# Second attention of a two-block transformer kernel: fp32 scores on 64 rows, the bias tile read from DRAM and added in the pass that takes the maximum, three SBUF tiles

## The reference

```python
def block(args):
    idx, qc = args
    q_pos = idx * Q_BLOCK + jnp.arange(Q_BLOCK)
    rel = k_pos[None, :] - q_pos[:, None]
    bias = rel_bias[t5_causal_bucket(rel)].astype(f32).transpose(2, 0, 1)
    s = jnp.einsum("bqhcd,bkhcd->bhcqk", qc, k).astype(f32) * scale
    s = s + bias[None, :, None]
    s = jnp.where(rel <= 0, s, NEG_INF_2)
    pm = jax.nn.softmax(s, axis=-1)
    attn = pm[:, :, 0] - lam * pm[:, :, 1]
    return jnp.einsum("bhqk,bkhe->bqhe", attn.astype(v.dtype), v)
```

## Time and profile before

| | |
|---|---|
| median of 3 runs | 2324.82 us (2322.73 to 2328.4) |
| profiled execution, its time | 2324.46 us |
| its span in the trace | 2322.7 us |
| mean granted TensorE clock | 0.955 of 2.4 GHz |
| busy share of PE, PEld, DVE, ACT, POOL | 92%, 72%, 55%, 35%, 20% |
| K and V projections | 1541.1 to 1666.7 us |
| second attention | 1669.7 to 1804.2 us |

### The profile page before, as it was taken

How to read it: one execution, slowest core, us unless ns; L and a number is a source line. 1 busy time by engine, 2 the same in 40 slices (tenths; PEclk the granted TensorE clock), 3 DMA queues, 4 the chain that set the end, 5 groups by cost and what they waited for, 6 DMA issues and landing times.

```text
span 2322.7 us, 27094 instructions
## 1 busy us (share of the span) xinstructions
PE 2128.9 (92%) x9788; PEld 1681.1 (72%) x9788; DVE 1281.0 (55%) x1733; ACT 819.9 (35%) x1309; POOL 466.5 (20%) x596
## 2 busy tenths in 40 slices
PE   8999999999999454799999999999977899999999
PEld 8987668888887354687787877665655577877877
DVE  4253356464355698347747466633366467556455
ACT  3123333122235345534424234432144344334233
POOL 4052017970015784010000001100131000000000
PEclk9999989999999777899999999999899899999999
DMA  4220022232322100122222323221100122323222
GB/s 141 90 73 1 1 73 91 91 100 90 100 91 74 35 1 1 65 91 82 91 99 90 109 82 104 89 69 63 59 19 10 46 82 91 109 80 106 79 98 100
DMA packets 48592, 172.16 MB, mean 74 GB/s; under 512 B 5806, under 2 KB 6318, under 8 KB 48492
## 3 DMA queue, kind: packets, MB, share of 16 engines
q1 hardware_dynamic: 47164, 166.46, 21.6%
q0 software_dynamic: 1328, 4.37, 0.6%
HBM read 168.68 MB, written 2.12 MB: 74 GB/s over the span
## 4 chain that ended last, share of the span: by engine, by line
PE 84%; DVE 8%; ACT 5%; issue 2%; POOL 0%; DMA 0%; DVEq 0%; SPq 0%; ACTq 0%; POOLq 0%
PE ps L393 65%; PE ps L555 6%; PE ps L517 2%; ACT sq L1061 2%; PE ps L1390 1%; PE ps L499 1%; DVE t L1075 1%; PE ps L690 1%; ACT u_t L839 1%; PE ps L691 1%; PE ps L711 1%; PE ps L1392 1%; PE ps L1410 1%; ACT t L1458 1%; PE ps L1026 1%
## 5 line engine op out<-in xcount | busy, mean ns | idle before, releaser
L393 PE MATMUL ps<-x_hi,w_hi 128*128 128x512 f32 x1280 | 513.2, 401 | 5.0 <-DVE w_lo L379 4.9
L393 PE MATMUL ps<-x_lo,w_hi 128*128 128x512 f32 x1280 | 507.1, 396 | 0.0
L393 PE MATMUL ps<-x_hi,w_lo 128*128 128x512 f32 x1280 | 506.4, 396 | 0.0
L379 DVE TENSOR_TENSOR w_lo<-raw,w_hi 128x1024 fp32r<-128x1024 f32 x308 | 395.6, 1287 | 165.1 <-ACT w_hi L375 165.1
L375 ACT ACTIVATE w_hi<-raw 128x1024 fp32r<-128x1024 f32 x308 | 321.8, 1049 | 308.0 <-PE ps L393 136.6
L393 PE MATMUL ps<-a_hi,w_hi 128*128 128x512 f32 x928 | 372.0, 401 | 19.1 <-DVEq L360 11.2
L393 PE MATMUL ps<-a_hi,w_lo 128*128 128x512 f32 x928 | 369.6, 398 | 0.0
L393 PE MATMUL ps<-a_lo,w_hi 128*128 128x512 f32 x928 | 369.5, 398 | 0.0
L393 PEld LDWEIGHTS ps<-x_hi,w_hi 128*128 128x128 f32 x1280 | 241.1, 188 | 86.4 <-issue 22.2
L445 POOL TENSOR_TENSOR t<-t,sq 128x512 f32<-128x512 f32 x49 | 71.4, 1456 | 1116.0 <-ACT sq L436 1115.0
L393 PEld LDWEIGHTS ps<-x_lo,w_hi 128*128 128x128 f32 x1280 | 241.3, 189 | 56.8 <-issue 1.7
(11 more groups left out here) (322 smaller groups left out, 2704.7 us busy)
## 6 DMA issues: line engine op xcount, KB each, us to landing
raw<-in_wstream SPq DMA_DIRECT2D x308, 512.0 KB, 3.3
h<-in_xT SPq DMA_DIRECT2D x4, 528.0 KB, 7.3
b_raw<-scratch POOLq DMA_DIRECT2D x8, 256.0 KB, 3.5
out<-h SPq DMA_DIRECT2D x8, 256.0 KB, 2.0
p_raw<-in_pT POOLq DMA_DIRECT2D x2, 512.0 KB, 4.6
b_in_<-in_ssm_bc POOLq DMA_DIRECT2D x1, 512.0 KB, 4.3
c_raw<-in_ssm_bc POOLq DMA_DIRECT2D x1, 512.0 KB, 6.2
vecs<-in_vecs SPq DMA_DIRECT2D x1, 294.0 KB, 3.8
```

Of the source, the lines that this page charges most:

```text
L379: e.tensor_tensor(w_lo[:, u.slot, :], raw[:, u.c % 2, :], w_hi[:, u.slot, :], ALU.subtract)\
L393: last = e.matmul(ps[:, bank, :], wt[:, u.slot, w], x[:, k0 + k, 0:SEQ], start=(k == 0 and n == 0), stop=(k == kt - 1 and n == 2))
```

## The change

The scores are one fp32 product per half on that half's 64 rows of `q2` and `k2`, with no staging; the scale 1/8 goes into the gain of the query's norm (`gain_q`). The bias no longer passes through TensorE. GpSimd writes each head's row 128 times to DRAM, at a pitch of 641, so that a read at a pitch of 640 gives the 128x512 tile in the right order of rows; two buffers `bias0`, `bias1` hold such tiles. `dve_top` adds bias and score, writes the negated sum to one of three SBUF tiles and takes the minimum in the same instruction; the exponential runs in place on that tile. The mix takes both reciprocals in one instruction of two columns. TensorE's step g is now scores(g), turn(g-2), pv(g-3); VectorE's is top(g), mix(g-1). The output goes to `v2`. What follows reads it there.

```diff
+    lam_pair = sb("lam_pair", [P, 2])
+    gain_q = sb("gain_q", [P, 1])
+        bias1 = sb("bias1", [P, SEQ], F32, c)
-            b_raw = sb("b_raw", [P, 1, SEQ], F32, cc)
+            bias0 = sb("bias0", [P, SEQ], F32, cc)
-    scratch = nc.dram_tensor("scratch", (8, 640), F32, kind="Internal").ap()
+    scratch = nc.dram_tensor("scratch", (8, P * 641), F32, kind="Internal").ap()
...
     def bias_load(e, p):
-        ge(e, blo_ok, p)
-        src = bass.AP(scratch.tensor, scratch.offset + p * 640 + 1, [[1, P], [1, SEQ]])
-        e.dma_start(b_raw[:, 0, :], src).then_inc(b_in, 16)
+        if p >= 2:
+            e.wait_ge(nb_ok, 32 + 8 * (p - 1))
+        src = bass.AP(scratch.tensor, scratch.offset + p * P * 641 + P, [[640, P], [1, SEQ]])
+        e.dma_start((bias0, bias1)[p % 2][:, :], src).then_inc(b_in[p % 2], 16)
+
+    def bias_rows(e, p):
+        dst = bass.AP(scratch.tensor, scratch.offset + p * P * 641, [[P * 641, 1], [641, P], [1, 640]])
+        e.dma_start(dst, tab[p:p + 1, :].unsqueeze(1).to_broadcast([1, P, 640])).then_inc(tab_out, 16)
+
+    ST = (t0, t1, t2)
...
         def pe_scores(g):
-            ge(e, exp_ok, 32 + 2 * (g - 1))
+            if g >= 2:
+                e.wait_ge(nb_ok, 32 + 2 * (g - 1))
             for c in range(2):
-                o = ps[:, 2 * sl + c, 0:N]
-                e.matmul(o, qs2[:, p % 2, c, qt * P:(qt + 1) * P], ks2[:, p % 2, 0:N], start=True, stop=False)
-                for n, t in enumerate((b_hi, b_lo)):
-                    last = e.matmul(o, flip_r[:, :], t[:, p % 2, SEQ - N:SEQ], start=False, stop=(n == 1))
+                r = slice(HD * c, HD * c + HD)
+                last = e.matmul(ps[:, 2 * sl + c, 0:N], q2[r, p, qt * P:(qt + 1) * P], k2[r, p, 0:N],
+                                start=True, stop=True)
             last.then_inc(s_mm, 1)
...
         def dve_top(g):
+            k = 2 * (g % 3)
             e.wait_ge(s_mm, 32 + g + 1)
+            if qt == 0:
+                e.wait_ge(b_in[p % 2], 16 * (p // 2 + 1))
+            if g >= 3:
+                e.wait_ge(pt_mm, 32 + g - 2)
             for c in range(2):
-                e.reduce_max(small[:, 1, 2 * sl + c:2 * sl + c + 1], ps[:, 2 * sl + c, 0:N], AX_X, negate=True)\
-                    .then_inc(nb_ok, 1)
+                e.tensor_tensor_reduce(ST[g % 3][:, c, 0:N], ps[:, 2 * sl + c, 0:N], (bias0, bias1)[p % 2][:, SEQ - N:SEQ],
+                                       -1.0, 3e38, ALU.add, ALU.min, small[:, 1, k + c:k + c + 1]).then_inc(nb_ok, 1)
...
         def dve_mix(g):
-            e.wait_ge(exp_ok, 32 + 2 * g + 1)
-            n = dve.did(e.reciprocal(r[0], small[:, 2, 2 * sl:2 * sl + 1]))
-            e.wait_ge(dve_did, n)
-            dve.did(e.tensor_scalar(t0[:, sl, 0:N], t0[:, sl, 0:N], r[0], None, ALU.mult))
             e.wait_ge(exp_ok, 32 + 2 * g + 2)
-            n = dve.did(e.reciprocal(r[1], small[:, 2, 2 * sl + 1:2 * sl + 2]))
+            n = dve.did(e.reciprocal(small[:, 3, k:k + 2], small[:, 2, k:k + 2]))
             e.wait_ge(dve_did, n)
-            n = dve.did(e.tensor_tensor(r[1], r[1], neg_lam[:, :], ALU.mult))
+            n = dve.did(e.tensor_tensor(small[:, 3, k:k + 2], lam_pair[:, :], small[:, 3, k:k + 2], ALU.mult))
...
         for p in range(8):
+            bias_rows(e, p)
+        e.wait_ge(tab_out, 16 * 8)
+        bias_load(e, 0)
+        fence(e, 5)
+        for p in range(1, 8):
             bias_load(e, p)
-            if p == 0:
-                e.wait_ge(hn_y, 17)
-                e.wait_ge(unit_ev, U_KV + 9)
-            stage2_pool(e, p)
-            if p == 0:
-                fence(e, 5)
```

More of the change, by code:

```diff
@@ L147, in build @@
         ptm = sb("ptm", [META, 2, P], F32, c)
[L148 to L155, removed]
     sb("region_a", [P, 2 * KT * SEQ])
@@ L196, in build @@
         x_s = sb("x_s", [P, 2, 4, P + 1], F32, c)
+    with ExitStack() as c:
+        vtok = sb("vtok", [P, 2, 4, P], F32, c)
+        pt2 = sb("pt2", [P, 2, 4, P], F32, c)
+        bias1 = sb("bias1", [P, SEQ], F32, c)
     sb("region_x", [P, 2 * KT * TOK])
@@ L333, in build @@
     tab_out = sem("tab_out")
-    b_in = sem("b_in")
-    bhi_ok = sem("bhi_ok")
-    blo_ok = sem("blo_ok")
+    b_in = [sem(f"b_in{k}") for k in range(2)]
     lam_v = sem("lam_v")
@@ L1352, in normed, with bias_load, pe_values @@
                 last(m - 1)
-    def stage2_pool(e, p):
-        par = p % 2
-        k = 4 * p
+    def bias_load(e, p):
         if p >= 2:
[L1358 to L1369, removed]
-        ge(e, blo_ok, p)
-        src = bass.AP(scratch.tensor, scratch.offset + p * 640 + 1, [[1, P], [1, SEQ]])
-        e.dma_start(b_raw[:, 0, :], src).then_inc(b_in, 16)
-    def attention2(e, who):
+            e.wait_ge(nb_ok, 32 + 8 * (p - 1))
[5 more added lines that the diff above has]
+    ST = (t0, t1, t2)
+    def attention2(e, who):
+        def pe_values(p):
+            ge(e, o_ok, p - 1)
+            for j in range(4):
+                last = e.transpose(ps[:, 6 + p % 2, j * P:(j + 1) * P], v2[:, p, j * P:(j + 1) * P], ident[:, :])
+            last.then_inc(vt_mm, 1)
         def pe_scores(g):
@@ L1447, in dve_out @@
         def dve_out(p):
             e.wait_ge(pv_mm, 32 + 4 * p + 4)
[L1449 to L1450 removed]
+            e.tensor_copy(v2[:, p, :], ps[:, 6 + p % 2, :]).then_inc(o_ok, 1)
         def act_exp(g):
[L1453 to L1460 removed]
@@ L1462, in act_turn @@
-        def act_turn(g):
-            p, qt, sl = g // 4, g % 4, g % 2
-            N = (qt + 1) * P
-            if qt == 0:
-                e.wait_ge(vt_mm, 4 + p + 1)
-                e.activation(vtok[:, p % 2, :, :].rearrange("p j c -> p (j c)"), ps[:, 6 + p % 2, :], ACT.Copy)\
-                    .then_inc(v2_ok, 1)
+            N = (g % 4 + 1) * P
+            t, k = ST[g % 3], 2 * (g % 3)
+            for c in range(2):
+                e.wait_ge(nb_ok, 32 + 2 * g + c + 1)
+                e.activation(t[:, c, 0:N], t[:, c, 0:N], ACT.Exp, bias=small[:, 1, k + c:k + c + 1], scale=-1.0,
+                             accum_out=small[:, 2, k + c:k + c + 1]).then_inc(exp_ok, 1)
@@ L1514, in _ @@
         load_unit(sp, Unit(1))
-        for name, t in (("spread", spread1), ("ident", ident), ("flip", flip), ("mask", mask), ("win", win)):
+        for name, t in (("spread", spread1), ("ident", ident), ("mask", mask), ("win", win)):
             sp.dma_start(t[:, :], A[name]).then_inc(consts_in, 16)
@@ L1873, in _ @@
         e.wait_ge(dve_did, n)
-        n = dve.did(e.tensor_scalar(neg_lam[:, :], small[:, 2, 0:1], -LAM, None, ALU.add))
+        dve.did(e.memset(lam_pair[:, 0:1], 1.0))
+        n = dve.did(e.tensor_scalar(lam_pair[:, 1:2], small[:, 2, 0:1], -LAM, None, ALU.add))
         fence(e, 5)
```

103 lines of the change are left out of this document (38 added, 65 removed).

## The result

| | before | after |
|---|---|---|
| median of 6 runs on the same chip | 2324.33 us | 2331.74 us (2329.99 to 2333.51) |
| ratio, with its 95% interval | | 1.0029 (1.0016 to 1.0041) |
| profiled execution, its time and span | 2324.46, 2322.7 us | 2329.99, 2328.2 us |
| second attention opens at | 1669.71 us | 1723.38 us |
| from there to the end of its last copy | 134.5 us | 87.9 us |

A forecast was written before the change was run, and what follows sets the result against it. The bound was taken as a loop through three engines, one query tile deep, no engine full. Second attention from 134.5 to 96.4 us saves 38.1, less 4 for the clock: 34.1 off 2324.5 gives 2290, range 2276 to 2316.

The forecast's parts named there:

- The failed step: K and V projections: bias row writes on GpSimd's queue beside the weight loads, with no time lost in the forecast.
- rival B: K and V projections: row writes slow the weight loads, up to 31 us lost, about 2308 us; chance 0.16.
- The price: Row writes before the second attention: between 11 and 243 us in all, with 129 us until the fence.
- Rival D: Fence before the second attention: row writes reach it late, at the high bound 116 us, giving 2407; chance 0.06.
- Rival E: Second attention: new passes give back what the loop gains, pipeline not deeper in effect, 2322 us; chance 0.02.
- The loop: Second attention, three tiles deep: 11.4 us a head, 91.2 for eight, 96.4 with start and end.
- Fused pass: VectorE's bias-add and reduction: 0.751 us at 512 columns, 4.41 a head; low bound 0.645 at 512.
- Rival C: VectorE's fused pass runs at half rate: 2.7 us more a head, 17 us in all, 2307; chance 0.14.
- TensorE's scores: Second attention's score products on 64 rows at the old price without overlap: 0.86 us for 512 columns, 4.3 a head.
- Its rival sum: Score halves in different row groups overlap: 2.2 to 3.3 us a head, sum about 5 lower; kept in the range.
- VectorE's waits and the clock: Second attention: VectorE waits 0.8 us once a head, for scores at 384 columns; slow clock costs 4 us.
- The sum: Second attention: 11.4 us a head, VectorE's work 10.6 of it; eight heads with start and end 96.4.

The follow-up runs named there:

- e1: Changed kernel without the row writes: small bias table stored reversed, the fused pass reading the tile's columns backwards; 2277.32 us, ratio 0.9787 to the kernel before.
- e4: Kernel before, with the eight row writes added to a DRAM tensor nobody reads and GpSimd waiting for them; 2386.88 us, ratio 1.0257.
- e3: Changed kernel, same row writes but row i read from partition i of another tile, so the bias is wrong; 2277.5 us in one run.
- e12: Changed kernel, GpSimd waiting for each row write to land before issuing the next (second run of this version); 2276.88 us, ratio 0.9794 to the kernel before.
- e8: e1 with the old shallow order: TensorE scores(g), turn(g-1), pv(g-2), VectorE mix(g-1), top(g); 2304.37 us, ratio 0.9906 to the kernel before.
- e7: e1 with both halves of the scores taken from the same 64 rows; 2297.13 us, ratio 0.9861 to the kernel before.
- e9: e1 with two fp32r products of 128 rows put ahead of each score, which overwrites them; 2318.04 us, ratio 0.9968 to the kernel before.
- e10: e1 with each head's output copy moved from VectorE to ScalarE; 2270.37 us, ratio 0.9759 to the kernel before.

## Why the prediction was wrong

**The failed step: what the row writes do to the weight loads, put at nothing.** The forecast took the row writes as hidden, since they end before the fence, and so gave their effect on the loads no term; rival B, in which they slow the loads, had 31 us at most. The runs showed 53.7 us in its place (e1, e4).

- *The price was not what failed.* The writes took 92 us, between the bounds of 11 and 243 and well under half of the latter, and they were over before the fence, as forecast. The Trainium skill ("SBUF — State Buffer", Door 1: The DMA port swizzle) gives 27.6 GB/s for partitions behind one port, from which the prediction had estimated 95 us; the trace agrees with its 28.4 GB/s, and e3, the same bytes from 128 partitions in 13 us, points the same way. The prediction added to that estimate that the engines would be held for all of it, and drew nothing from it for the loads.
- *The sharing.* Rival B let each weight packet wait for one packet of the row writes. With the 2.16 us measured for such a packet its own formula gives a load in 3.2 + 8 x 2.16 = 20.5 us, however many writes are queued (by the earlier trace rows a load has 9 packets an engine, which gives 22.6). Measured were 14.3 behind one, 24.6 behind two, 48.7 behind four and up to 75.1 behind eight; 4 loads were asked for in 95 us. The term of 31 us was 53.7.
- *The point from which it decides.* The prediction set the argument "only 20% of the engines' time is used" against B. e12 has the engines as full as the kernel after (93% and 94% with both queues), and loses nothing. Not the share decided, but how many writes are queued when a load is asked for.

Rival D, the fence waiting for the row writes, didn't happen: they were done at about 1635, and the fence opened at 1723 for want of weights. With a term of 53.7 for the row writes the prediction's own sum would have been 2290 + 54 = 2344, on the other side of 2324; the attention gave back 12.5 of these, and what follows it 1.6. Rival E has 2322, near the measured time, but by a loop that gains nothing, and this one gained 46.6 us.

**The loop, right and mis-sized.** The forecast was 96.4 us, plus 4 for the clock; it took 87.9. The order of the engines does what was said: ScalarE's 66.1 us for the maxima are 2.3, and e8 puts the depth's worth at 27 us. At the full clock, for which the forecast was made, a head takes 9.7 us instead of 11.4. Its terms, from the timeline of VectorE and the groups by shape:

```profile
1731.05 0.68 DVE L1406 CUSTOM_DVE_ANT_0 t<-ps,bias 128x512 f32<-128x512 f32 x1
1731.66 0.08 DVE L1406 DVE_READ_ACCUMULATOR2_ANT small<- 128x1 f32 x1
1731.66 0.69 DVE L1406 CUSTOM_DVE_ANT_0 t<-ps,bias 128x512 f32<-128x512 f32 x1
```

```profile
L1406 DVE CUSTOM_DVE_ANT_0 t<-ps,bias 128x512 f32<-128x512 f32 x16 | 10.3, 684 | 0.0
...
L1417 DVE TENSOR_SCALAR t<-t,small 128x512 f32<-128x512 f32 x8 | 3.9, 487 | 0.3
```

- *Fused pass.* Taken at 0.751 us for 512 columns, measured 0.684, and the next one starts 0.61 behind it, as the reductions did (1.29 for two). The read of the accumulator, 0.08, is hidden. From the four sizes' starts (0.61, 0.49, 0.35, 0.21) a head's eight passes take 3.3 us, not 4.41: the low bound was right and I took the middle. Rival C, half rate, is out. The rule of the Trainium skill that the prediction cited ("Vector Engine (DVE) Microarchitecture Reference", Points that are easy to get wrong) speaks of two sources in SBUF, and with one of them in PSUM the trace shows no halving.
- *Mixing.* The scale at 512 columns was taken at 0.49, without GpSimd's staging: 0.487. Right.
- *TensorE's scores.* 4.3 us a head without overlap was wrong. The chain shows the four passes of 384 columns at 0.87, where 1.30 was taken, beside products as forecast:

```profile
1747.22 0.67 PE ps L1392 x6
1747.89 0.87 PE ps L1374 x4
```

The rule of the Trainium skill on row groups that the prediction cited and set aside ("TensorE: Matmul & The Clock Gate", Part 3: Packing small matmuls) holds nearly in full, 0.57 to 0.59 of the time on the same rows, where a full overlap would be a half. Its rival sum, 5 us less, was the better one.
- *VectorE's waits and the clock.* Two forecasts, and both came out nearly right. VectorE was to wait once a head, 0.8 us for the scores at 384 columns; at the full clock it waits there alone, for 0.60 us (1748.78). The clock was to cost 4 us. The stage has it at full for long stretches with short ones at half:

```profile
1737.00:1754.00 17.00, 13.61 (x89) 8.89 (x87) 15.11 (x58) 11.86 (x36) 1.10 (x2) 1.00 0.05 16
1754.50:1757.50 3.00, 3.00 (x13) 2.12 (x13) 1.88 (x7) 1.74 (x6) 0.00 (x0) 0.50 0.25 79
```

Such a short stretch falls into every second head, and there VectorE waits in a second place, for the scores at 256 columns. So the heads take 9.7 and 10.8 us by turns, and the longer ones cost 3 to 4 us in all. The rows of the first of them, with the clock at 0.50 up to 1737:

```profile
1736.77 0.42 DVE L1406 CUSTOM_DVE_ANT_0 t<-ps,bias 128x256 f32<-128x256 f32 x1 [0.75 <-PE ps L1374]
...
1739.07 0.56 DVE L1406 CUSTOM_DVE_ANT_0 t<-ps,bias 128x384 f32<-128x384 f32 x1 [0.55 <-PE ps L1374]
```

VectorE is busy 15.1 of 17 us at the full clock, 89%, near the 90 forecast, and 70.1 of 87.9 in the whole stage.
- *The sum.* A head is 1.7 us shorter than forecast at the full clock, 1.5 of it VectorE's own work, 9.1 us instead of 10.6, and 0.2 the wait. Eight times 1.7 is 13.6, about the 12.5 by which the stage is shorter than 100.4.

The parts don't add: depth 27, products and halves apart 42, 46.6 gained in all. Each experiment takes one away, makes another engine the bound, and changes the clock with it.

## What to carry to other kernels

Price a transfer by how many partitions its source spans, and then, even if it is done in time, ask what is asked for behind it: two or more slow transfers queued at once delayed the loads that TensorE lives on, while the same transfers, each asked for when the last had landed, cost nothing. A small table need not be copied into the shape that a read wants either; here it could be stored reversed and read backwards in the same time. When a stage with no full engine loops through three of them, one more tile of depth is worth a lot (27 us of 115 here), and after it the price of single instructions on the fullest engine counts again. And compare the lengths of a repeated piece at the same granted clock, or the clock's share is taken for the engine's.

## What the runs showed of the hardware

- A transfer of 320 KB out of one partition takes 13.6 us by itself (e12), some 2.2 us a packet on each engine (4 KB), 15 times a packet of the weights. A weight load of 3.7 us landed after 14.3 behind one of them and after 24.6 behind two. Why the hardware queue gets so few turns among such packets isn't shown by any run; with one write queued at a time it got 1440 packets through in 95 us, with eight 531.
- The granted clock did not follow how busy TensorE was: busy for 55 us on end and granted 0.50 (e7), busy for 29 us on end and granted 0.50, and then busy 87.5 of 90 us and granted 1.00 (e9), busy 51.1 of 61 us and granted 1.00 (e10). What lets it rise there stays open.
- Two fp32 products of 64 rows on different rows of the array take 0.57 (512 columns) and 0.59 (384) of their time on the same rows (after, e7), if no other product stands between them (e9).
- A VectorE pass that reads one operand backwards takes the time of one that reads it forwards (0.685 and 0.684 us).
